# Sparse experts on one Trainium2 core: from 64 blocks of 128 rows to 48 blocks of two 64-row halves

## What is computed

```python
def hier_moe(h, moe_w):
    ...
    gate = top_p / jnp.sum(top_p, -1, keepdims=True) * p_grp
    expert = grp[:, None] * EXPERTS_PER_GROUP + top_i.astype(jnp.int32)
    ...
    def run_block(args):
        xb, e = args
        return (jax.nn.silu(xb @ w_eg[e]) * (xb @ w_eu[e])) @ w_ed[e]
    ...
    return jnp.zeros((T, D), h.dtype).at[tok].add(y_a)

def trunk_layer(...):
    ...
    f = hier_moe(h.reshape(B * S, D), moe_w).reshape(B, S, D)
    y = layer_norm(DN_ALPHA * h + f, ln2_g, ln2_b)
```

## Time and profile before

| | us |
|---|---|
| median of 3 executions | 3192.64 (3190.05 to 3194.82) |
| span of the profiled execution | 3185.8 |
| PE busy | 2883.6 (91%) |
| DVE busy | 1738.2 (55%) |
| ACT busy | 970.2 (30%) |
| POOL busy | 522.3 (16%) |
| first gate matmul of the experts' stage to that of the last block | from 2430.01 to 3097.16 |
| combine | from 3129.57 to the end |

### The profile page before, as it was taken

One profiled execution on the slowest core, in us unless ns is written; L12 is line 12 of the kernel. 1 busy time (PEld: TensorE's weight loads), 2 busy tenths in 40 slices (PEclk: granted clock), 3 DMA queues, 4 the chain that ended last, 5 costly groups with the idle time before them and its releaser, 6 DMA issues. The chain is left out here.

```text
span 3185.8 us, 65923 instructions
## 1 busy us (share of the span) xinstructions
PE 2883.6 (91%) x26600; PEld 2202.1 (69%) x26600; DVE 1738.2 (55%) x3821; ACT 970.2 (30%) x2497; POOL 522.3 (16%) x554
## 2 busy tenths in 40 slices
PE   7999999999999999669899898989976999999990
PEld 6888888888888888545555555545545777777770
DVE  1666666666666666558686868822235222222225
ACT  2333333333333333234343434412220111111116
POOL 0000000000000000010000000011113554545540
PEclk9999999999999999689999999999988999999995
DMA  6211111222111211420101010033335899886447
GB/s 196 37 38 37 37 37 38 40 39 39 37 38 39 42 38 37 93 88 1 39 1 39 1 36 1 1 127 132 126 110 210 282 336 325 278 279 177 97 93 251
DMA packets 337225, 310.23 MB, mean 97 GB/s; under 512 B 235200, under 2 KB 290528, under 8 KB 322528
## 3 DMA queue, kind: packets, MB, share of 16 engines
q1 hardware_dynamic: 315424, 238.88, 24.5%
q0 software_dynamic: 21504, 67.13, 9.1%
HBM read 208.12 MB, written 84.42 MB: 92 GB/s over the span
## 5 line engine op out<-in xcount | busy, mean ns | idle before, releaser
L814 PE MATMUL mx_bank<-mx_xT,mx_w_in 128*128 128x128 f32 x5168 | 646.4, 281 | 16.9 <-DVEq L281 13.4
L814 PEld LDWEIGHTS mx_bank<-mx_xT,mx_w_in 128*128 128x128 f32 x5168 | 600.8, 193 | 60.5 <-issue 36.2
L2311 DVE STREAM_TRANSPOSE ex_xT<-ex_x 128x256 f32<-128x256 f32 x256 | 141.5, 610 | 332.3 <-DMA ex_x<-scr_hx,ex_idx 332.3
L1497 PE MATMUL at_bank<-pl_kT,pl_qT 128*128 128x512 f32 (+5 forms) x656 | 289.9, 528 | 2.3 <-issue 2.3
L1469 ACT ACTIVATE at_PQ<-at_bank,at_nms 128x512 f32<-128x512 f32 (+5 forms) x328 | 192.7, 595 | 252.9 <-DVE at_nms L1597 251.5
L2159 POOL DMA_INDIRECT ex_x<-scr_hx,ex_idx x256 | 244.9, 957 | 114.8 <-issue 77.7
L2242 PE MATMUL ex_gate<-pl_wg,ex_xT 128*128 x1024 | 233.6, 381 | 13.7 <-DVE ex_xT L2311 11.4
L2242 PEld LDWEIGHTS ex_gate<-pl_wg,ex_xT 128*128 128x128 f32 x1024 | 195.1, 191 | 68.7 <-issue 44.9
L2266 PE MATMUL ex_down<-pl_wd,ex_hT 128*128 x512 | 230.3, 592 | 1.5 <-ACT ex_hT L2194 1.5
L2242 PE MATMUL ex_up<-pl_wu,ex_xT 128*128 x1024 | 231.6, 379 | 0.0
L1528 PEld LDWEIGHTS at_bank<-at_PT,at_vals 128*64 128x64 f32 (+1 forms) x2208 | 117.4, 136 | 151.5 <-issue 78.1
(11 more groups left out here) (310 smaller groups left out, 4480.2 us busy)
## 6 DMA issues: line engine op xcount, KB each, us to landing
pl_wg<-in_w_eg SPq DMA_DIRECT2D x32, 1024.0 KB, 6.1
pl_wu<-in_w_eu SPq DMA_DIRECT2D x32, 1024.0 KB, 10.3
pl_wd<-in_w_ed SPq DMA_DIRECT2D x32, 1024.0 KB, 14.3
mx_x<-in_x SPq DMA_DIRECT2D x76, 128.0 KB, 3.7
pl_ro_x<-in_x SPq DMA_DIRECT2D x17, 512.0 KB, 4.2
scr_hx<-ro_h SPq DMA_DIRECT2D x17, 512.0 KB, 2.6
scr_acc<-ro_ha SPq DMA_DIRECT2D x17, 512.0 KB, 3.1
co_r<-scr_acc SPq DMA_DIRECT2D x17, 512.0 KB, 5.6
```

What stands on the lines that cost most here:

```text
L814: ins = pe.matmul(dst, w_in[:, k, col:col + n], xT[:, k, :], start=(k == 0), stop=(k == KC - 1))
L1497: t.mark(pe.matmul(bank[n % SB][:, 0:wd], qT[h][keys(h), j * P:(j + 1) * P], kT[h][keys(h), k0 * P:k0 * P + wd], start=True, stop=True), f ...
L2311: ins = v.transpose(xT[s][:, :, 32 * h:32 * h + 32], x[s][:, h, :].rearrange("p (i k) -> p k i", k=KC))
```

## The change

The unit becomes a half of 64 rows. There are at most 96 halves, paired into 48 blocks. The two halves of a block may belong to different experts. Experts that have no assignment are left out: experts are numbered by `rank` among those in use.

- PE computes the two halves of each product on the two column halves of its array: `out[0:64]` from the first half's rows and weights, `out[64:128]` from the second half's. The transposes become ordinary matmuls with the identity, 64 stationary columns each.
- The second half's weights are not read from their slot but from a fixed copy: DVE copies the second half's `wg` and `wu` (128x2048 each) into `bg` and `bu` for every block, ACT copies `wd` into `bd`. These copies have one buffer each.
- A token whose two experts are in the same block stands twice in one add. Its second row goes to a second accumulator, the upper half of `acc`, which `router` now fills with zeros (17 stores more) and `combine` adds to the first: for each tile POOL clears `c`, gathers the marked rows of the second accumulator (indices of all others are out of bounds and skipped), and adds columns 0 to 511; DVE adds the others.
- SP loads `wg`, `wu` of a rank when `up` of the slot's last block is done and `wd` when its `down` is done. The first four ranks are loaded in dispatch, but only once DVE has written which experts they are (`first_used`).
- POOL's order in experts is now: gathers of block i+2, then add(i). DVE's is: transposes of block i+1, silu(i), copy `bg` for i+1, hidden(i), copy `bu` for i+1.
- `down(i)` on PE waits for `y` of block i-1; there are two `down` banks as before.

The core of the diff:

```diff
-NBLK = (ASSIGN + NE * (P - 1)) // P
+HB = P // 2
+NSUB = (ASSIGN + NE * (HB - 1)) // HB
+NBLK = NSUB // 2
...
-        blank_out = Dmas(nc, ctx, "ro_blank_out", 2)
+        blank_out = Dmas(nc, ctx, "ro_blank_out", 2 + NT + 1)
...
+                blank_out.go(sp.dma_start(second[col, :], blank[:]))
...
+            sp.wait_ge(first_used, 1)
             for s in range(SLOTS):
-                sp.sem_inc(weights.w_in[s].sem, 16 * weights.w_in[s].n)
-                load_expert(sp, io, weights, s, bass.ds(s, 1))
+                e = bass.ds(sp.value_load(keep["free_at"][0:1, s:s + 1], min_val=0, max_val=NE - 1), 1)
+                load_expert_in(sp, io, weights, s, e)
+                load_expert_out(sp, io, weights, s, e)
...
-            do(v.tensor_tensor(cmp1[:], bc(counts, KB), bm(nums[:, 0:KB], NE), ALU.is_gt))
-            do(v.tensor_reduce(blocks[:], cmp1[:], AX.X, ALU.add))
+            do(v.tensor_scalar(blocks[:], counts, 1.0 / HB, 0.5 - 0.5 / HB, ALU.mult, ALU.add))
+            rounded(blocks[:])
+            do(v.tensor_scalar(live[:], blocks[:], 1.0, None, ALU.min))
...
+                do(v.tensor_tensor(pair[:, n0:n1, 2, :], at_block[:, n0:n1, :], bc(again[:, n0:n1], NBLK), ALU.mult))
...
+            for r in range(NE):
+                if r >= SLOTS:
+                    e = bass.ds(sp.value_load(keep["free_at"][0:1, r:r + 1], min_val=0, max_val=NE - 1), 1)
+                    groups = sp.value_load(groups_of[0:1, r - SLOTS:r - SLOTS + 1], min_val=1, max_val=NBLK)
+                    sp.wait_ge(up_done, groups)
+                    load_expert_in(sp, io, given, r % SLOTS, e)
...
+                if r >= SLOTS:
+                    sp.wait_ge(down_done, groups)
+                    load_expert_out(sp, io, given, r % SLOTS, e)
...
             for i in range(2):
-                for s in range(2):
-                    gathers(i, s)
-            for i in range(turns):
-                for s in range(2):
-                    add(i, s)
-                    if i < turns - 2:
-                        gathers(i + 2, s)
+                gathers(i)
+            for i in range(NBLK):
+                if i + 2 < NBLK:
+                    gathers(i + 2)
+                add(i)
...
+            def second_out(i):
+                e = rank(a, 2 * i + 1)
+                at = slot(a, e)
+                a.wait_ge(out_ready, a.snap(e + 1))
+                a.activation(bd[:], flat(wd[:, at, :]), ACT.Copy).then_inc(bd_made, 1)
...
                 for k in range(KC):
-                    ins = pe.matmul(b[s][:, 0:FE], xT[s][:, k, :], wv[:, k * FE:(k + 1) * FE], start=(k == 0), stop=(k == KC - 1))
+                    c = slice(k * FE, (k + 1) * FE)
+                    pe.matmul(out[s][0:HB, 0:FE], xT[s][:, k, 0:HB], wv[:, c], start=(k == 0), stop=(k == KC - 1))
+                    ins = pe.matmul(out[s][HB:P, 0:FE], xT[s][:, k, HB:P], b[:, c], start=(k == 0), stop=(k == KC - 1))
+                return ins
+
+            def gate(i, e, at):
+                pe.wait_ge(xT_made, i + 1)
+                pe.wait_ge(in_ready, pe.snap(e + 1))
+                pe.wait_ge(bg_made, i + 1)
...
+            for i in range(NBLK):
+                more = i + 1 < NBLK
                 if more:
+                    turned(i + 1)
+                silu(i)
+                if more:
+                    at = second_gate(i + 1)
+                hidden(i)
+                if more:
+                    second_up(i + 1, at)
...
+        @block.gpsimd
+        def _(g):
+            def bring(t):
+                k = t % NB
...
+                g.memset(c[k][:], 0.0).then_inc(cleared, 1)
+                g.wait_ge(cleared, t + 1)
+                g.indirect_dma_start(c[k][:], None, scr["acc"], bass.IndirectOffsetOnAxis(ap=keep["rows"][:, t:t + 1], axis=0),
+                                     bounds_check=2 * (TOK + P) - 1, oob_is_err=False).then_inc(c_in[k], 16)
+
+            for t in range(NB):
+                bring(t)
+            for t in range(NT):
...
+                g.tensor_tensor(r[k][:, 0:LOW], r[k][:, 0:LOW], c[k][:, 0:LOW], ALU.add).then_inc(low_summed, 1)
+                if t + NB < NT:
+                    bring(t + NB)
```

More of the change, by code:

```diff
@@ L1985, in _ @@
             ins.then_inc(counted, 1)
+            pe.wait_ge(columns, 1)
+            for k in range(3):
+                ins = pe.matmul(turned[0:32, k * P:(k + 1) * P], bcol[:, k, :], ident, start=True, stop=True)
+            ins.then_inc(turns, 1)
             for k, (n0, n1) in enumerate(PARTS):
@@ L2250, in up @@
[L2250 to L2263 removed]
+            pe.wait_ge(ident_in, 16)
@@ L2299, in _ @@
-            past = Turn(pe, down, turns - 1)
-            at1 = slot(expert(2 * turns - 1))
-            turned(past, 1)
-            hten.whole()
-            result(past, 1, at1)
-            down.whole()
+                        c = slice(m * D + n * 512, m * D + (n + 1) * 512)
+                        pe.matmul(down_b[n][0:HB, :], hT[s][:, m, 0:HB], wv[:, c], start=(m == 0), stop=(m == FC - 1))
+                        ins = pe.matmul(down_b[n][HB:P, :], hT[s][:, m, HB:P], bd[:, c], start=(m == 0), stop=(m == FC - 1))
@@ L2306, in _, with turned @@
+                ins.then_inc(down_done, 1)
+            before = None
+            for i in range(NBLK):
+                e = rank(pe, 2 * i)
+                at = slot(pe, e)
+                gate(i, e, at)
+                if i > 0:
+                    turned(i - 1)
+                up(i, at)
+                if i > 0:
+                    down(i - 1, *before)
+                before = e, at
+            turned(NBLK - 1)
+            down(NBLK - 1, *before)
         @block.vector
         def _(v):
-            def turned(t, s):
-                t.arrived(x_in[s])
+            def turned(i):
+                s = i % 2
+                v.wait_ge(x_in[s].sem, x_in[s].done(i // 2))
+                if i >= 2:
+                    v.wait_ge(up_done, i - 1)
@@ L2330, in _, with second_gate @@
-            v.tensor_copy(idx[:], keep["onehot"][:, NBLK:5 * NBLK]).then_inc(listed, 1)
-            for own in (vec, xt):
-                v.sem_inc(own.sem, own.per)
-            for s in range(2):
-                turned(Turn(v, xt, 0), s)
-            xt.whole()
-            for i in range(turns - 1):
-                turn(i, True)
-            turn(turns - 1, False)
+                ins.then_inc(xT_made, 1)
+            def second_gate(i):
+                e = rank(v, 2 * i + 1)
+                at = slot(v, e)
+                v.wait_ge(in_ready, v.snap(e + 1))
+                if i > 0:
+                    v.wait_ge(gate_done, i)
+                v.tensor_copy(bg[:], flat(wg[:, at, :])).then_inc(bg_made, 1)
+                return at
```

395 lines of the change are left out of this document (204 added, 191 removed).

## The result

The changed kernel takes 3283.5 us (median of 4 runs, 3272.8 to 3287.3), the kernel before 3191.4 beside it: a ratio of 1.0285, with a 95% interval of 1.0265 to 1.0306. It is slower, as forecast, but by 92 us and not by 29, and just above the range. The profiled execution has a span of 3281.9 us, 96.1 more than before.

| stretch | before | after | more | forecast |
|---|---|---|---|---|
| span's start to gate 0 (dispatch, first gathers) | 2430.0 | 2443.4 | +13.4 | +8 |
| gate 0 to the last gate (63 steps; 47 steps) | 667.2 | 708.9 | +41.7 | -7 |
| last gate to combine's first load | 32.4 | 32.0 | -0.4 | 0 |
| combine | 56.3 | 97.7 | +41.4 | +28 |

The account below looks back on a forecast made before the run. PE was taken to bound the experts' stage before, a two-block ring of waits after. Experts -7 (-60 ring, +26 clock, +27 copies), combine +28, dispatch +4, first gathers +4: +29 on 3192.6, 3222 us; range 3165 to 3280.

Parts of the forecast that it names:

- PE's work: Experts: two half-width matmuls run side by side, so a block takes PE 10.81 us instead of 10.57.
- The ring: Experts: waits from one `down` through result, add, gathers, transposes, copy and gate to `down` two blocks on: 26.25 us, unfilled 25.54.
- The alternation: Experts, sign in the profile: gate starts alternate between about 10.8 and 15 to 18 us.
- The landing: Experts, fourth gather's issue to the transposes' start: 3.5 us for filled blocks, 2.79 for unfilled ones.
- rival of late gathers: Experts: filled blocks' gathers keep landing 6.31 us after issue, 52 us more, 3274; chance 0.22 together with POOL stopped by copies.
- the stopped POOL: Experts, rival: each copy holds POOL for its whole length, 27 us more, 3250; chance 0.22 together with late gathers.
- The clock: Experts: after idling PE runs the gate product at half clock, 1.2 us a ring, +26 us.
- Copies against POOL: Experts: DVE's `bg` and `bu` copies delay POOL's add and gathers, 1.25 us a ring, +27; upper bound +55.
- Unfilled rings: Experts, two-block turns without weight loads under way: 25.54 us, plus 1.2 for clock and 1.25 for copies.
- Combine: Combine stage: first total after 13.2 to 16.7 us, 12 tiles at 3.6 to 4.3 us each; +28 us in all.
- Dispatch: Before gate 0: small DVE steps add 4 us, first gathers falling into the later first weight loads another 4.
- Waits for weights: Experts: PE waiting for weights priced at nothing, because four slots still lead by more than three blocks.

Follow-up runs that it names:

- the third buffer: The changed kernel with three x buffers instead of two in experts, so gathers of block i+3 precede the add of block i: 3088.7 us.

## Why the prediction was right or wrong

- **PE's work.** 10.81 us a block forecast, 10.78 measured once PE ended last again. The halves run side by side.
- **The ring.** Right: its path and its releasers in the page. The alternation came from block 17 on, and not as 10.8 and 15 to 18 us between gates but as 12 to 15 and 15 to 22, because the gate at half clock lengthens the short step too. Without the landing, the clock and the copies every term is within 0.1 us.
- **The landing is the step that failed.** "Now two of the three go out already at the end of `up`. I take 3.5 for filled blocks, near the free end". The loaded row stood right beside it: 6.31, and 6.33 is the mean over the filled blocks of that trace; measured 6.49, which is 3.0 us in each of 18 rings, 54 us. The run with all loads at the end of `down` shows that the argument was empty (6.62); the run with an eighth of the bytes shows that it is the weights' bytes (3.21, and 65 us less in the stage). What I overlooked is in the order of PE: `up` of the next block stands ahead of `down`, so the loads of the ring's time fall around its gathers either way. 2981.52 and 2989.01 in the turn above are one of each. This was my rival of late gathers, with 52 us for it; I gave it 0.22 together with the stopped POOL. The Trainium skill, "DMA: Bandwidth & Descriptors", section "Queues, rings and completion order", says that each DMA engine takes turns between the queues that have work, a packet at a time; the gathers (software queue) and the loads (hardware queue) are two of them, and the runs agree with it as far as they show that a gather isn't held for a whole load (6.5 us, where `wu` needs 11.1) and isn't free of it either.
- **The clock.** Mechanism right, 1.2 us a ring too little: 1.60 on the mean of the 24 filled blocks that waited (nothing in five of them, 1.4 to 3.0 in the others), 1.7 in unfilled rings. The price did not follow the length of the idle stretch: 1.7 us behind 3.8 us of idle (block 46), 1.7 behind 8.5 (block 18), 2.7 behind 8.4 (block 36). The unfilled pairs with PE kept busy confirm the price there.
- **Copies against POOL.** Right that they hold it, wrong in the price on the ring: 0.4 us, not 1.25. What I called "just while DVE copies" held mostly for the other block of the pair. The section "SBUF: two separate sides" of "SBUF — State Buffer" in the Trainium skill has the mechanism, and the trace agrees with it: 2.37 us for a gather beside two copies, 0.95 alone, and 0.96 on the mean when the copies are left out. The +55 us that it would have given count every copy as if it lay on the ring.
- **Unfilled rings.** 25.54 + 1.2 + 1.25 = 28.0 forecast, 27.5 measured.
- **Combine.** First total 15.3 us in, within 13.2 to 16.7. The tile was mis-sized: 3.6 to 4.3 forecast, 4.68 measured, since 0.2 us of semaphores between clear and gather are 0.77 and the sum takes 1.27. Over 12 tiles that is 5 to 13 us. The gather's issue was at the upper of my two rows, 1.60 us for 1.00 where DVE stood idle. "The last five have no clear and run at the old pace" is wrong as well; POOL's last two sums wait for r tiles (0.15 and 6.04 us). Together +41 in place of +28: 10.8 at the start, 25.1 for the 12 tiles, 5.5 at the end. That is just over the 40 that I had named for POOL and DVE holding each other up, and they do.
- **Dispatch.** +4.7 for the steps (4 forecast; 42.4 us from dispatch's first step to the first gather in every kernel with the new dispatch, 37.7 before), +6.6 for the first gathers (4 forecast). The weights under way are 3.4 us of landing and 5.4 us in all by the run that loads them early. The other 2.1 us lie ahead of dispatch; they are inside the 2379.5 to 2388.2 between which dispatch starts in kernels of the same code, so neither they nor the router's 17 stores of zeros show a cost of the change.
- **Waits for weights.** None, as forecast, not even with the third buffer, where the loads of 28 experts fall into some 430 us.

With 6.31 for the landing the sum would have been 3274, some 9 us from the truth. Part of that would have been luck: the copies, priced about 19 us too high over 22 rings, would have covered much of what the clock (9), combine (13) and dispatch (5) cost more than I had given them. I had the row and argued it away.

## What to carry to other kernels

Fewer and fuller steps helped here only once everything that is prefetched per step had its lead in time again: one step less of lead, with the same buffers, turned a wholly busy TensorE into one that waits 7 us in every second block, and one more buffer of 4 KB per partition gave back 191 us of the stage. When a transfer's landing has a free and a loaded price in the trace, take the loaded one unless a row shows the load gone at that very moment. A helper engine that clears, gathers and sums per tile can leave most of that to a gather with an add; then give it tiles enough to cover its landing.

## What the runs showed of the hardware that I had not expected

- A gather that brings hardly a row (0.02 to 0.03 MB for 17 of them) still takes 5.6 us to land in the median in combine, and 6.0 with an add. The add isn't what makes it slow: in the run that clears once, the same plain gathers land in 2.6 us in the median. There POOL issues them some 2 us behind the load of an r tile, and 1.2 us ahead of one in the changed kernel; no run separates the two.
- POOL needs 0.77 us between a clear and the bounds-checked gather behind it, also with DVE and ACT idle (two of 0.77 us between 3189 and 3195), and 0.30 between two gathers in experts.
- DVE's steps with two SBUF inputs and POOL's work hold each other up: 2.77 for 1.28 us on DVE beside POOL's sum and clear, 1.60 for 1.00 on POOL's gather beside DVE's steps.
- Half of the 128 columns at a time, alternating between two weight sources, costs PE nothing: 10.78 us a block with 64-column pieces, 10.57 with full ones, and the 0.2 is the turn (from its start to that of `up` 0.44 us, 0.23 before).
